# The DeltaNet layer's opening re-ordered: gate sums directly behind the first k projection, modulation moved behind the first N, and a and b projected in four column groups

## Chip, core and metric

The kernel runs on one core of a Trainium2 chip. The metric is the device time of one execution in microseconds (us), lower is better. A core has five instruction queues that run side by side and meet only at semaphores: PE (TensorE, matrix multiplications; "PEld" is its weight load), DVE (VectorE), ACT (ScalarE), POOL (GpSimd) and SP (SyncE, which only issues DMAs here). All data and all matrix products are float32.

## What is computed

Two layers over 256 latent tokens and 256 context tokens of width 1024. Layer 0 mixes by pooling, layer 1 by a bidirectional gated DeltaNet; each is followed by a mixture of experts. Every sub-layer is scaled, shifted and gated by a modulation vector. What the change touches is the entry into layer 1:

```python
def modulation(cvec, w_mod, b_mod):
    m = jax.nn.silu(cvec) @ w_mod + b_mod          # 1024 -> 6 * 1024, for each layer
    return jnp.split(m, 6, axis=-1)

def gdn_mixer(h, w_in, conv_w, a_log, dt_bias, ...):
    proj = h @ w_in                                # q, k, v, z: 1024 wide each; a, b: 16 each
    qkv = short_conv(proj[..., :3072], conv_w)     # 5 taps along the tokens, then SiLU
    g = -jnp.exp(a_log) * jax.nn.softplus(a + dt_bias)
    beta = jax.nn.sigmoid(b)
    ...                                            # per head and direction, in chunks:
    g = jnp.cumsum(g, -1)
    decay = exp(where(tril, g[i] - g[j], -inf))
    A = where(strict, (k * beta) @ k.T * decay, 0)
    sol = triangular_solve(eye + A, rhs)           # the inverse that the kernel builds
    ...                                            # then a recurrence over the chunks
```

There are 8 heads and 2 directions; the kernel works in 4 chunks of 128 tokens, so it inverts 8 triangular 128x128 systems for each head.

## The kernel before

**One head of the DeltaNet.** A head goes through: projections of k, v, q and z (`pe_project(h, j)` with j = 0 for k, 1 for v, 2 for q; `pe_project_z`), convolution (`dve_conv`), SiLU (`act_conv`), k times k transposed and k turned into rows (`pe_keys`), the exponents of the decays (`dve_n_args`, line 1189) and their Exp (`act_exp_n`, line 1196), the product N (`dve_n`, line 1232). N's diagonal 32x32 blocks are copied out (line 1239 on DVE, 1247 on ACT), sent to memory and read back in another layout by SP (`sp_blocks_out`, line 1004; `sp_blocks_in`, lines 1008 and 1010), and inverted row by row on POOL (`pool_invert`, lines 1033 to 1040). The result goes to memory and back (`sp_inverse_out`, line 1014; `sp_inverse_in`, line 1021), DVE and ACT place it (lines 1317 and 1358), and PE joins the blocks to inverses of 64 and 128 (`pe_join32`, line 1329, and what follows), after which the recurrence over the chunks runs (`pe_recur`).

**Steps.** Heads are pipelined by a step number x. Each engine has a function for a step (`pe_step`, `act_step`, `dve_step`, `sp_step`). In step x the engines make head x+1 up to its N and, beside it, close head x (join, recurrence). Step -1 makes head 0 alone; on PE it is not `pe_step` but a list of calls written out in the block at the end. PE's step 0 begins with the v projection of head 1 (`pe_project(1, 1)`), and everything there comes before the join of head 0. The order on each engine is the order in which the code is written; nothing re-orders it.

**Before the steps.** `pe_dn_setup` turns the modulated rows into columns `m.hT`, projects a and b (line 1710: 8 matmuls over the contraction in 8 parts, each 32 output rows wide and 512 tokens long), ACT copies the result (line 1738), PE turns it back to tokens in rows (line 1714). DVE and ACT form the gates (lines 1775 to 1784 and 1740 to 1745). `pe_dn_cumulate` sums them along the tokens by three matmuls (line 1721), DVE reads the sums (lines 1788 to 1800), PE turns them (line 1725), ACT copies them (line 1749), SP writes them to memory (line 1853) and reads them back spread over all partitions as `along` (line 996). `dve_n_args` needs `along`.

**Modulation.** The modulation of a layer is made in 3 groups q of 2048 columns, each in 8 parts k. For each part SP loads 1 MB of weights into a ring slot (`sp_mod`, line 239), PE multiplies in four column groups of 32 (`pe_mod`, line 251: 4 matmuls), DVE adds the bias (`dve_mod`, line 268), PE spreads the vector over the partitions (`pe_mod_spread`, line 262: 4 matmuls in banks 1 and 2) and ACT copies it (`act_mod`, line 274). The last two groups are q = NQ+1 and q = NQ+2 (NQ is 3). For q = NQ+2 only ring slots 4 and 5 are free, so part k+2 is loaded only when PE has used part k (`mod_before`). PE begins step 0 only when all copies are made, since the joins use banks 1 and 2:

```python
            pe_mod_spread(pe, NQ + 2, 1)
            pe.wait_ge(s("mod_ready"), 2 * NCH)
            for x in range(HEADS + 1):
                pe_step(pe, x)
```

SP, after step -1, waits until all modulation matmuls are done before it loads the second half of the output weights (line 1861) and only then comes to step 0, whose first act is the store of head 0's inverse.

## Time and profile before

| | us |
|---|---|
| median of 3 runs | 1050.08 (1046.65 to 1051.48) |
| the profiled execution | 1047.63 |
| its span in the profile | 1045.8 |
| PE busy | 810.4 (77%) |
| PE weight load busy | 482.5 (46%) |
| DVE busy | 428.5 (41%) |
| POOL busy | 384.2 (37%) |
| ACT busy | 330.1 (32%) |

The profiled execution takes 1.8 us more than its span, and 2.5 us less than the median. PE is the busiest engine, but the program has stages with different limits, so the shares of the whole span say little about one stage. The stage in question lies between about 398 us (columns `m.hT` ready) and 540 us (blocks of head 2 leave for memory). A timeline row gives the start in us, the duration in us, engine, line, operation, operands and, in brackets, the idle time before it and what ended it. PE splits each float32 matmul into two records, so x16 there is 8 matmuls.

### The profile page before, as it was taken

Reading aid. Unit: us, or ns where it says so; the run is one execution under the profiler, and the core shown is the slowest. Engines: PE = TensorE matmul, PEld = TensorE weight load, DVE = VectorE, ACT = ScalarE, POOL = GpSimd, SP = SyncE. Lnnn points to the kernel's source line nnn. Section 1 sums busy time; section 2 is a strip of 40 time slices with the busy share of each in tenths; the row PEclk is TensorE's granted clock in tenths of the full one; section 3 lists DMA queues with packets and bytes.
Section 4 is the critical chain, followed back from the end, with each engine's and each line's share of the span. In section 5 each row is a group of like instructions: output and inputs, shape, how many; then the busy total and the mean of one; then the engine's idle time right before and its main releaser. Section 6 shows DMA issues by size and latency. Waiting matters only on the chain.

```text
span 1045.8 us, 14887 instructions
## 1 busy us (share of the span) xinstructions
PE 810.4 (77%) x5183; PEld 482.5 (46%) x5183; DVE 428.5 (41%) x1005; ACT 330.1 (32%) x760; POOL 384.2 (37%) x718
## 2 busy tenths in 40 slices
PE   4498655999999158687799989899856863999980
PEld 0255332555555013254566666666645432555540
DVE  0306651111111692153576665676643333111115
ACT  0131202222222214054374564654741012222221
POOL 0000771333333395016438346364370022533330
PEclk8599766999999568688798898998965876899995
DMA  9999199968593694645523515334220346799933
GB/s 355 343 418 396 43 398 367 382 246 291 214 379 134 259 348 146 229 122 168 137 41 102 138 20 126 72 76 137 41 82 10 121 180 263 259 376 383 381 127 121
DMA packets 113533, 220.44 MB, mean 211 GB/s; under 512 B 44469, under 2 KB 78589, under 8 KB 100543
## 3 DMA queue, kind: packets, MB, share of 16 engines
q1 hardware_dynamic: 101272, 199.71, 54.6%
q0 software_dynamic: 8224, 15.75, 4.5%
q10 hardware_dynamic: 3975, 4.16, 1.2%
q8 instruction: 38, 0.62, 0.2%
q14 instruction: 24, 0.20, 0.1%
HBM read 213.25 MB, written 17.33 MB: 220 GB/s over the span
## 4 chain that ended last, share of the span: by engine, by line
PE 38%; POOL 18%; DMA 15%; DVE 11%; issue 11%; ACT 3%; SPq 3%; ACTq 1%; DVEq 0%; POOLq 0%
PE banks L656 11%; POOL arena L1039 7%; POOL arena L1037 7%; PE banks L668 6%; DMA weight_ring<-in_w_mod_dram 4%; DMA inverted_blocks<-arena 3%; PE banks L1810 3%; PE banks L1057 3%; PE banks L637 3%; SPq L1010 2%; PE banks L251 2%; DMA arena<-blocks 2%; DMA blocks<-arena 2%; POOL x_rows L319 2%; PE banks L834 2%
## 5 line engine op out<-in xcount | busy, mean ns | idle before, releaser
L1057 PE MATMUL banks<-h_cols,weight_ring 128*128 128x512 f32 (+1 forms) x384 | 163.6, 558 | 1.5 <-ACT modulation L274 0.7
L759 POOL DMA_INDIRECT y_of_tokens<-arena,place_now x42 | 44.4, 1056 | 161.4 <-ACT arena L691 157.3
L715 DVE TENSOR_TENSOR arena<-arena,banks 128x128 f32<-128x128 f32 x42 | 12.1, 288 | 211.7 <-ACT arena L684 162.2
L251 PE MATMUL banks<-weight_ring,c_cols 128*32 128x512 f32 x384 | 64.4, 776 | 42.4 <-DMA weight_ring<-in_w_mod_dram 42.2
L1057 PEld LDWEIGHTS banks<-h_cols,weight_ring 128*128 128x128 f32 x384 | 71.7, 204 | 40.4 <-issue 35.3
L1039 POOL TENSOR_TENSOR arena<-arena 128x60 f32<-128x60 f32 (+10 forms) x240 | 79.7, 332 | 18.8
L1037 POOL TENSOR_TENSOR arena<-arena 128x60 f32<-128x60 f32 (+10 forms) x240 | 76.9, 320 | 18.8
L735 POOL DMA_INDIRECT arena<-h_of_tokens,row_now x50 | 48.5, 970 | 69.4 <-POOL row_now L762 22.8
L679 ACT COPY arena<-arena 64x1024 f32<-64x1024 f32 x46 | 48.1, 1045 | 76.3 <-PE banks L637 54.1
L725 POOL DMA_DIRECT2D h_of_tokens<-h_rows x6 | 3.9, 646 | 183.1 <-DVE h_rows L307 183.1
L1033 POOL TENSOR_TENSOR arena<-arena,const 128x256 f32<-128x256 f32 x8 | 6.7, 843 | 168.6 <-DMA arena<-blocks 168.6
L656 PE MATMUL banks<-weight_ring,arena 128*64 128x256 f32 x544 | 66.6, 401 | 2.3 <-ACT arena L679 2.3
L637 PE MATMUL banks<-const,arena 64*128 64x64 f32 x352 | 57.0, 285 | 12.4 <-ACT arena L679 12.4
L637 PEld LDWEIGHTS banks<-const,arena 64*128 64x128 f32 x352 | 45.2, 198 | 35.3 <-issue 21.0
L656 PEld LDWEIGHTS banks<-weight_ring,arena 128*64 128x64 f32 x544 | 41.1, 145 | 31.1 <-issue 8.3
L684 ACT ACTIVATE arena<-banks 128x128 f32<-128x128 f32 x42 | 11.7, 278 | 127.1 <-PE banks L656 127.1
L319 POOL TENSOR_SCALAR x_rows<-x_rows,small 128x1024 f32<-128x1024 f32 x10 | 46.2, 4618 | 13.4 <-DVE small L301 13.0
L251 PEld LDWEIGHTS banks<-weight_ring,c_cols 128*32 128x32 f32 x384 | 9.9, 122 | 84.6 <-DMA weight_ring<-in_w_mod_dram 44.7
L709 DVE COPY arena<-banks 128x512 f32<-128x512 f32 x44 | 30.4, 691 | 35.6 <-PE banks L637 35.4
L1098 DVE SCALAR_TENSOR_TENSOR h_rows<-arena,h_rows 128x512 f32<-128x512 f32 (+1 forms) x64 | 41.0, 640 | 1.6
L274 ACT COPY modulation<-banks 128x512 f32<-128x512 f32 x24 | 13.1, 587 | 73.0 <-PE banks L262 37.9
L691 ACT COPY arena<-banks 128x512 f32<-128x512 f32 x42 | 24.6, 587 | 32.9 <-PE banks L668 32.9
(283 smaller groups left out, 1550.6 us busy)
## 6 DMA issues: line engine op xcount, KB each, us to landing
weight_ring<-in_w_mod_dram SPq DMA_DIRECT2D x48, 1024.0 KB, 10.8
weight_ring<-in_dn_w_in_dram SPq DMA_DIRECT2D x32, 512.0 KB, 7.1
weight_ring<-in_w_gate_dram SPq DMA_DIRECT2D x14, 1024.0 KB
weight_ring<-in_w_up_dram SPq DMA_DIRECT2D x14, 1024.0 KB
weight_ring<-in_w_down_dram SPq DMA_DIRECT2D x14, 1024.0 KB
arena<-in_w_gate_dram SPq DMA_DIRECT2D x6, 1024.0 KB
arena<-in_w_up_dram SPq DMA_DIRECT2D x6, 1024.0 KB
arena<-in_w_down_dram SPq DMA_DIRECT2D x6, 1024.0 KB
```

Source lines behind the costliest of these rows:

```text
L251: mm = pe.matmul(m.ps[j * COL:(j + 1) * COL, 0, :], m.c_cols[:, k, :], w[:, j, :], start=(k == 0), stop=(k == KD - 1))
L319: pool.tensor_scalar(x, x, v.mean_var[:, n % 4, 0:1], v.rstd[:, n % 4:n % 4 + 1], ALU.subtract, ALU.mult).then_inc(s("ln_gained"), 1)
L637: mm = pe.transpose(m.ps[:, B_TURN, k * TILE:(k + 1) * TILE], v.rows[:, k, :], v.ident[0:TILE, 0:TILE])
L656: mm = pe.matmul(column_half(B_GU, h)[:, 0:2 * P], v.slots_T[:, k, :], gate_up(slot, k)[:, :, h * P:(h + 1) * P], start=(k == 0), stop=(k ...
L668: mm = pe.matmul(column_half(B_DOWN, h), v.hidden[:, f, :], down(slot, f)[:, h * BANK:(h + 1) * BANK], start=(f == 0), stop=(f == FC - 1))
L679: act.copy(v.rows_flat, v.rows_in[u]).then_inc(s(t_ + "rows_copied"), 1)
L735: pool.indirect_dma_start(v.rows_in[u], None, h_dram, bass.IndirectOffsetOnAxis(m.row_now[:, at:at + 1], 0), bounds_check=last_token, oob_ ...
L759: pool.indirect_dma_start(y_halves, bass.IndirectOffsetOnAxis(m.place_now[:, u:u + 1], 0), v.y_tile[u], None, bounds_check=last_row, oob_i ...
L1037: then(pool.tensor_tensor(part, U[:, 0:q, j:j + 1].to_broadcast([P, q, BLK - 1 - j]), M[:, j, j + 1:BLK].unsqueeze(1).to_broadcast([P, q, ...
L1039: then(pool.tensor_tensor(U[:, 0:q, j + 1:BLK], U[:, 0:q, j + 1:BLK], part, ALU.subtract))
L1057: mm = pe.matmul(bank(6 + j % 2)[:, 0:CTX + SEQ - n0], head_w[h % 2][:, j, k, :], m.hT[:, k, n0:CTX + SEQ], start=(k == 0), stop=(k == KD ...
L1098: ins = dve.scalar_tensor_tensor(out=out, in0=src, scalar=tap, in1=out, op0=ALU.mult, op1=ALU.add)
```

## The change

Seven edits, all in the opening of layer 1:

- a and b: the 8 contraction parts are spread over four column groups of 32, so that each group sums two parts in its own 32 of the 128 output rows. The copy then takes 128 rows, and the turning back is a matmul with a new 128x32 constant that adds the four groups.
- The matmuls of the gate sums stand directly behind head 0's k projection, and the turning of the sums behind two more matmuls (of the v projection).
- `pe_keys(0)` stands inside the v projection, behind its part 5.
- The spread of group NQ+1 and the parts of group NQ+2 move behind: parts 0 and 1 before the z projection, 2 and 3 behind head 0's values, the spread of NQ+1 behind head 1's k projection, and parts 4 to 7 behind that.
- SP loads parts 2 to 7 of group NQ+2 after head 0's blocks have landed, no longer before and around the gate rows.
- ACT makes the copies of group NQ+1 after step -1, and in step -1 the copy of v's projection (`act_pad(0, 1)`) behind the Exp of N's exponents.
- DVE makes the convolution of head 0's k before N's exponents.

The order on PE, from the projection of a and b to the first keys of head 1. Line 251 is a modulation part (4 matmuls each), 262 the spread, 1057 a projection (128x512 for k and v, 128x256 for q), 1066 z, 1721 and 1725 the gate sums, 1111 and 1116 the keys, 1138 the values. Before:

```order
L1710 MATMUL banks<-h_cols,dn_inputs 32x512 x8
L1714 MATMUL banks<-const,arena 128x32 x4
L1057 MATMUL banks<-h_cols,weight_ring 128x512 x8
L262 MATMUL banks<-mod_sums,const 128x512 x4
L251 MATMUL banks<-weight_ring,c_cols 32x512 x8
L1057 MATMUL banks<-h_cols,weight_ring 128x512 x8
L251 MATMUL banks<-weight_ring,c_cols 32x512 x8
L1721 MATMUL banks<-arena,const 128x64 x3
L1725 MATMUL banks<-const,arena 64x128
L251 MATMUL banks<-weight_ring,c_cols 32x512 x8
L1111 MATMUL banks<-const,arena 128x128 x4
L1116 MATMUL banks<-arena 128x128 x4
```

The same stretch of PE now (lines are one to seven higher: 1715 is 1710, 1727 is 1721, 1732 is 1725, 1112 is 1111):

```order
L1715 MATMUL banks<-h_cols,dn_inputs 32x512 x8
L1720 MATMUL banks<-const,arena 128x32 x4
L1058 MATMUL banks<-h_cols,weight_ring 128x512 x8
L1727 MATMUL banks<-arena,const 128x64 x3
L1058 MATMUL banks<-h_cols,weight_ring 128x512 x2
L1732 MATMUL banks<-const,arena 64x128
L1058 MATMUL banks<-h_cols,weight_ring 128x512 x3
L1112 MATMUL banks<-const,arena 128x128 x4
L1117 MATMUL banks<-arena 128x128 x4
L1058 MATMUL banks<-h_cols,weight_ring 128x512 x3
```

Between the k projection and the gate sums stood a spread, two modulation parts, the v projection and two more parts; now nothing does.

The end of PE's opening, from the values of head 0 to the beginning of step 0 (the five matmuls of line 1057, now 1058), before:

```order
L1138 MATMUL banks<-const,h_rows 128x128 x4
L1057 MATMUL banks<-h_cols,weight_ring 128x512 x8
L262 MATMUL banks<-mod_sums,const 128x512 x4
L1057 MATMUL banks<-h_cols,weight_ring 128x512 x5
L1111 MATMUL banks<-const,arena 128x128 x4
```

and now:

```order
L1139 MATMUL banks<-const,h_rows 128x128 x4
L252 MATMUL banks<-weight_ring,c_cols 32x512 x8
L1058 MATMUL banks<-h_cols,weight_ring 128x512 x8
L263 MATMUL banks<-mod_sums,const 128x512 x4
L252 MATMUL banks<-weight_ring,c_cols 32x512 x16
L263 MATMUL banks<-mod_sums,const 128x512 x4
L1058 MATMUL banks<-h_cols,weight_ring 128x512 x5
```

Six of the eight parts of group NQ+2 and a second spread now stand here, ahead of step 0.

SP around the same place (1004 to 1010 are the blocks of head 0, 996 is `along`, 991 the weights of head 2), before:

```order
L239 DMA weight_ring<-in_w_mod_dram 128x2048 [waits mod_mm] x4
L1853 DMA decay_rows<-arena 2x8x128 [waits dn_setup_rows]
L1853 DMA decay_rows<-arena 2x8x128 x3
L996 DMA x_rows<-decay_rows 128x1024 [waits x_moved,gc_rows]
L996 DMA x_rows<-decay_rows 128x1024
L239 DMA weight_ring<-in_w_mod_dram 128x2048 [waits mod_mm] x2
L1004 DMA blocks<-arena 128x8x32 [waits k_length,n_mat]
L1008 DMA arena<-blocks 128x8x32 [waits n_out]
L1010 DMA arena<-blocks 32x1024 x4
L991 DMA weight_ring<-in_dn_w_in_dram 128x8x128 [waits proj,m_in]
```

and now:

```order
L1859 DMA decay_rows<-arena 2x8x128 [waits dn_setup_rows]
L1859 DMA decay_rows<-arena 2x8x128 x3
L997 DMA x_rows<-decay_rows 128x1024 [waits x_moved,gc_rows]
L997 DMA x_rows<-decay_rows 128x1024
L1005 DMA blocks<-arena 128x8x32 [waits k_length,n_mat]
L1009 DMA arena<-blocks 128x8x32 [waits n_out]
L1011 DMA arena<-blocks 32x1024 x4
L240 DMA weight_ring<-in_w_mod_dram 128x2048 [waits mod_mm,m_in]
L240 DMA weight_ring<-in_w_mod_dram 128x2048 [waits mod_mm] x5
L992 DMA weight_ring<-in_dn_w_in_dram 128x8x128 [waits proj]
```

The six weight loads moved from in front of and behind the gate rows to behind the landing of the blocks (`m_in`).

The diff, cut to its core:

```diff
+    v.add_groups = c[:, C_SLOT * P + 96:C_SLOT * P + 128]
...
-        abT = exp_q.rearrange("p d n -> p (d n)")[0:2 * NV, :]
+        abT = exp_q.rearrange("p d n -> p (d n)")
...
                 sp.wait_ge(s("m_in"), 80 * (x + 2))
+            if x < 0:
+                sp_mod(sp, NQ + 2, 2, KD)
...
             if x < 0:
-                act_pad(act, x + 1, 1)
                 act_squares_k(act, x + 1)
                 act_exp_n(act, x + 1)
+                act_pad(act, x + 1, 1)
...
         def dve_step(dve, x):
-            if x < 0:
-                dve_n_args(dve, 0)
             if closed(x):
                 dve_q_args(dve, x)
             if made(x):
                 dve_conv(dve, x + 1, 0)
+            if x < 0:
+                dve_n_args(dve, 0)
...
-            for k in range(KD):
-                mm = pe.matmul(m.ps[0:2 * NV, 3, :], w_ab[:, k, :], m.hT[:, k, :], start=(k == 0), stop=(k == KD - 1))
+            for r in range(2):
+                for g in range(4):
+                    mm = pe.matmul(m.ps[g * 2 * NV:(g + 1) * 2 * NV, 3, :], w_ab[:, 4 * r + g, :], m.hT[:, 4 * r + g, :],
+                                   start=(r == 0), stop=(r == 1))
             mm.then_inc(s("dn_setup_mm"), 1)
             pe.wait_ge(s("dn_setup_rows"), 2)
             for t in range(TT):
-                mm = pe.transpose(bank(4)[:, t * 2 * NV:(t + 1) * 2 * NV], abT[:, t * P:(t + 1) * P],
-                                  v.ident[0:2 * NV, 0:2 * NV])
+                mm = pe.matmul(bank(4)[:, t * 2 * NV:(t + 1) * 2 * NV], abT[:, t * P:(t + 1) * P], v.add_groups,
+                               start=True, stop=True)
...
-        def pe_dn_cumulate(pe):
+        def pe_dn_cumulate(pe, beside):
...
             mm.then_inc(s("dn_setup_mm"), 1)
+            beside()
             pe.wait_ge(s("dn_gates"), 4)
...
-            act.copy(abT, m.ps[0:2 * NV, 3, :]).then_inc(s("dn_setup_rows"), 1)
+            act.copy(abT, m.ps[:, 3, :]).then_inc(s("dn_setup_rows"), 1)
...
-            sp_mod(sp, NQ + 2, 2, 6)
             sp.wait_ge(s("dn_setup_rows"), 3)
...
-            sp_mod(sp, NQ + 2, 6, KD)
             sp_step(sp, -1)
...
             act_dn_setup(act)
-            act_mod(act, NQ + 1)
...
             ln_loads(act, 1, 0)
+            act_mod(act, NQ + 1)
             act_mod(act, NQ + 2)
...
             pe_dn_setup(pe)
             pe_project(pe, 0, 0)
-            pe_mod_spread(pe, NQ + 1, 1)
+            pe_dn_cumulate(pe, lambda: pe_project(pe, 0, 1, 0, 2))
+            pe_project(pe, 0, 1, 2, V_FIRST)
+            pe_keys(pe, 0)
+            pe_project(pe, 0, 1, V_FIRST, KD)
             for k in (0, 1):
-                pe_mod(pe, NQ + 2, k)
-            pe_project(pe, 0, 1)
-            for k in (2, 3):
-                pe_mod(pe, NQ + 2, k)
-            pe_dn_cumulate(pe)
-            for k in (4, 5):
-                pe_mod(pe, NQ + 2, k)
-            pe_keys(pe, 0)
-            for k in (6, 7):
                 pe_mod(pe, NQ + 2, k)
             pe_project_z(pe, 0)
             pe_project(pe, 0, 2)
             pe_values(pe, 0)
+            for k in (2, 3):
+                pe_mod(pe, NQ + 2, k)
             pe_project(pe, 1, 0)
+            pe_mod_spread(pe, NQ + 1, 1)
+            for k in range(4, KD):
+                pe_mod(pe, NQ + 2, k)
             pe_mod_spread(pe, NQ + 2, 1)
             pe.wait_ge(s("mod_ready"), 2 * NCH)
...
+    c[:, C_SLOT * P + 96:C_SLOT * P + 128] = i % 32 == np.arange(32)[None, :]
```

## Rows read from the trace of the kernel before

**Rows 1.** Waits, 384 to 510 us: engine, line, releaser: total us, times, longest

```profile
DVE arena L1788 <- PE banks L1721: 19.1, 1, 19.1
```

**Rows 2.** Timeline of PE in the setup: start us, duration us, line, operands, records

```profile
398.39 7.05 PE L1710 MATMUL banks<-h_cols,dn_inputs 128*32 128x512 f32 x16
406.11 0.43 PE L1714 MATMUL banks<-const,arena 32*128 32x32 f32 x4 [0.67 <-ACT arena L1738]
406.47 7.13 PE L1057 MATMUL banks<-h_cols,weight_ring 128*128 128x512 f32 x16
...
429.07 1.93 PE L251 MATMUL banks<-weight_ring,c_cols 128*32 128x512 f32 x16
430.93 0.88 PE L1721 MATMUL banks<-arena,const 128*128 128x64 f32 x6
```

**Rows 3.** Timeline of DVE, the gates and the bias sum of group NQ+2

```profile
412.47 0.22 DVE L1782 SCALAR_TENSOR_TENSOR arena<-arena,dn_inputs 128x64 f32<-128x64 f32 x1
...
465.80 0.69 DVE L268 TENSOR_TENSOR mod_sums<-banks,mod_sums 128x512 f32<-128x512 f32 x1
```

**Rows 4.** Timeline of ACT: after the last setup Exp, and head 1's diagonal

```profile
435.15 1.28 ACT L1103 ACT_TABLE_LOAD   x1
...
485.72 0.81 ACT L1247 COPY arena<-arena 32x256 f32<-32x256 f32 x2
```

**Rows 5.** The chain that ended last, 340 to 500 us: start us, us, what

```profile
431.92 0.20 DVE arena L1788
...
442.56 1.66 DVE arena L1189 x8
444.21 0.41 DVE arena L1095
...
447.79 0.64 ACT arena L1103
...
452.56 0.64 ACT arena L1196
...
456.40 2.28 DMA blocks<-arena
...
465.80 0.74 POOL arena L1033
```

**Rows 6.** Timeline of PE from the v projection to the join of head 0

```profile
420.87 8.27 PE L1057 MATMUL banks<-h_cols,weight_ring 128*128 128x512 f32 x16
...
437.62 1.94 PE L251 MATMUL banks<-weight_ring,c_cols 128*32 128x512 f32 x8 [0.55 <-DMA weight_ring<-in_w_mod_dram]
...
470.13 1.13 PE L262 MATMUL banks<-mod_sums,const 2*128 2x512 f32 x4
471.93 1.61 PE L262 MATMUL banks<-mod_sums,const 2*128 2x512 f32 x4 [0.67 <-ACT modulation L274]
474.21 6.25 PE L1057 MATMUL banks<-h_cols,weight_ring 128*128 128x512 f32 x10 [0.68 <-ACT modulation L274]
...
488.73 1.89 PE L1057 MATMUL banks<-h_cols,weight_ring 128*128 128x256 f32 x8
501.07 1.06 PE L1329 MATMUL banks<-arena 32*32 32x32 f32 x32 [10.46 <-DVE arena L1317]
```

**Rows 7.** Issue to landing of line 239's loads, 418 to 442 us

```profile
DMA to landing us min/median/max: 4.8/6.5/9.4
```

**Rows 8.** Issue to landing of line 1861's load, second half of output weights

```profile
DMA to landing us min/median/max: 13.4/13.4/13.4
```

**Rows 9.** Timeline of SP's queue: inverse of head 0 out; blocks of heads 1, 2

```profile
491.89 0.56 SPq L1014 DMA_DIRECT2D inverted_blocks<-arena  x1
...
497.19 0.52 SPq L1004 DMA_DIRECT2D blocks<-arena  x1
...
539.04 1.45 SPq L1004 DMA_DIRECT2D blocks<-arena  x1
```

**Rows 10.** Stretch at the beginning of step 0: length, PE busy, PE clock, DMA, GB/s

```profile
472.00:476.00 4.00, 3.33 (x7) 0.80 1.14 331
```

## The prediction

> **What bounds the kernel now.** I read the waits first. DVE sat idle 19.1 us for the gate sums [rows 1], the longest wait of PE, DVE or ACT in this opening. The timeline of PE shows why: the sums (line 1721) stand at 430.93, though the gates they need were finished at 412.7 (DVE line 1782, 412.47 + 0.22) [rows 2, 3]. In between PE did a spread, two modulation parts, the v projection and two more parts. Then the chain of waits: from the first reading of the sums (431.92) it runs without a gap over `along` (442.56), the convolution of k (444.21), its SiLU (447.79), the Exps (452.56) and the blocks of head 0 (456.40) to POOL's first inversion (465.80) [rows 5]. POOL is done 26.1 us later (491.89) [rows 9], and PE, which had finished all it could do at 490.62, waits 10.46 us for head 0's inverse until 501.07 [rows 6]. So before that join the bound is the path to N and POOL, not PE. Two things leave this stage: blocks of head 1 at 497.19 and of head 2 at 539.04 [rows 9]; from there on the loop over heads repeats. What the change is worth is how much earlier the blocks of head 2 leave.
>
> **Part 1, a and b in column groups.** Before, 8 matmuls in 7.05 us. The modulation parts have this very shape and use four column groups: two parts, that is 8 matmuls, took 1.93 us [rows 2]. So 5.1 us are saved. The copy has four times the partitions and the same 512 elements in each, so it costs the same. Turning back took 0.43 us for four; three matmuls with a full 128x128 stationary took 0.88 [rows 2], so four take 1.1 to 1.2: 0.7 us lost. Net 4.4 us: head 0's k projection starts at 406.47 - 4.4 = 402.1 and ends 7.1 later, at 409.2; the gates are ready at 412.7 - 4.4 = 408.3, before that.
>
> **Part 2, sums behind k, up to POOL.** Sums at 409.2 to 410.1, first reading 410.2 instead of 431.92: 21.7 us earlier. Two v matmuls (0.9 each) stand before their turning and end 0.25 after DVE's results are due, so `along` follows at 410.2 + 0.25 + (442.56 - 431.92 = 10.64) = 421.1. The convolution of k no longer waits for that: it starts when ACT's setup Exps are done, which was at 435.15 [rows 4] and is now at 413.7, and takes 3.6 (444.21 to 447.79). SiLU at 417.3, and by the old distance of 4.8 us over keys and squares ACT is free for the Exps at 422.0. N's exponents take 1.65 us for eight from 421.1, the first four 0.8: 421.9. Both paths meet at 422.0. From the Exps to the blocks it was 3.84 us, now 0.4 more because two small DVE operations stand behind the exponents: 426.2. POOL 9.4 later: 435.6. Both are 30.2 earlier than before [rows 5]. That the v copy stands later on ACT costs nothing: its projection ends at about 423, and the z projection, which needs the copy, comes only after two modulation parts.
>
> **Part 3, the modulation now in the way.** The 30 us do not reach the end, because PE may not begin step 0 until all modulation is copied. SP loads parts 2 to 7 only after the blocks have landed, at 435.6; PE has by then done its values (about 436.5) and waits. With two slots the loads come in pairs: the first needs 4.8 us when nothing is queued [rows 7], the second lands 2.5 later (0.55 idle behind a part of 1.94) [rows 6]. Step by step: parts 2 and 3 landed 442.9; part 3 multiplied 1.9: 444.8; head 1's k projection 8.3, taking the row that was partly at 1.2 GHz [rows 6]: 453.1; the first spread 3.4 on PE (470.13 to 473.54) [rows 6]: 456.5; part 4 (its load came beside the projection) 1.0: 457.5; only now can part 6 be loaded, 4.8, and part 7, 2.5: 464.8; part 7 multiplied 1.9: 466.7; bias sum 0.8 with its hand-over [rows 3]; the last spread with copies 4.1 (470.13 to 474.21) [rows 6], with 0.4 added as PE will be at the lower clock: step 0 at 472.0. Before it was 474.21. So PE gains only 2.2 us there; six loads that were hidden now stand in a row.
>
> **Part 4, what comes out.** PE's work in step 0 up to the join took 16.4 us (474.21 to 490.62) [rows 6] and will be ready at 488.4. Head 0's inverse: POOL done 435.6 + 26.1 = 461.7; SP is held by its wait for all modulation (466.7) and the issue of the output weights (1.7), so the store goes at 468.5. It came back to a placed inverse 9.2 us after its issue (491.89 to 501.07) [rows 6, 9]: 477.7, before 488.4. PE no longer waits, so the 10.46 us go as well. From the join to the blocks of head 2 is 37.97 us: 526.4. The other path is head 1's: its diagonal was ready 12.3 us after the beginning of step 0 (485.72 + 0.81 - 474.21) [rows 4, 6], now at 484.3, and the blocks of head 2 follow 41.85 us behind those of head 1 (497.19 to 539.04) [rows 9]: 526.2. Both give 12.6 to 12.8 us. I take 1 us off for the clock: before, it was at 0.80 of full speed at the beginning of step 0 [rows 10] after dense work; now PE has been waiting for loads.
>
> Of that clock the Trainium skill ("TensorE: Matmul & The Clock Gate", Part 1) says that the slow state is the default and activity releases it. By that rule alone the five projection matmuls that open step 0 would run wholly at the low clock.
>
> The price from rows: 6.25 us before [rows 6], of which the low clock was a part; eight at full clock took 7.13 [rows 2], so five take 4.4 at 2.4 GHz and 8.9 at 1.2 GHz. All low would cost 2.6 us more than before, the full clock would return 1.8. I take 1.
>
> **SP's queue.** The store of head 0's inverse moves behind a freshly issued load of 2 MB, which took 13.4 us from issue to landing when head weights were queued ahead of it [rows 8], as they are now. If the store waits all of it: 466.7 + 13.4 = 480.1, plus at most the 9.2 = 489.3: PE's join waits 0.9 us. Head 1's blocks go right behind the reload, at about 485 to 486 rather than 484.3. So 1 us, 2 at most.
>
> The Trainium skill ("DMA: Bandwidth & Descriptors", Queues, rings and completion order) has descriptors of a ring consumed in order and the semaphore write only after every earlier write of that DMA engine. By it the sum would be a gain of about 10.6, by the rows of an unloaded queue 11.6; no row of the kernel before has this store behind a load.
>
> **Sum.** 12.6 - 1 = 11.6 us. Against the profiled execution: 1047.6 - 11.6 = 1036.0. The median lies 2.5 above it: 1050.1 - 11.6 = 1038.5.
>
> **Rivals.**
> 1. PE warm and loads short. If PE is at 2.4 GHz from part 3 on, the k projection takes 7.1 and nothing is added in step 0: 1.2 + 0.4 + 1 + 1.8 = 4.4 us more, a gain of 16: 1034. For it: even with a spread's waits just behind it, the clock at the beginning of step 0 was still 0.80 [rows 10]; against: it now waits three times for loads. Chance 0.14.
> 2. Column groups do not overlap. Then the 5.1 us return and pass through the whole path to step 0: gain 6.5, 1043.5. Against it stand the modulation parts with the same shape. Chance 0.03. With the store held longer than I take it, or the k projection and spreads at the low clock throughout (14 instead of 8.3 for the projection), the gain is likewise 5 to 8, 1042 to 1045: chance 0.11.
> 3. The gain is eaten inside the head loop. The two paths in part 4 are within 0.2 us of each other, so any delay on one of them counts in full, and what came for free in PE's idle 10.46 us (head 1's v convolution on DVE, for one) is now beside the join. If half of it returns: gain 1 to 5, 1045 to 1049. Chance 0.1.
> 4. Slower: the loads in pairs. Each pair stands on PE's path to step 0 with 7.3 us. The break-even is a step 0 at 472.0 + 11.6 = 483.6, that is 5.8 us more for each of the two pairs. The longest landing in the quiet stretch was 9.4 [rows 7]; the 13.4 of the big load is the bound from above [rows 8]. With 13.4 in place of 4.8, twice: 17.2 later, 5.6 us slower than before: 1055.7. Against: nothing else is in the queue when parts 2 and 3 are issued, and only head 2's weights follow parts 6 and 7. Chance 0.07.
> 5. As forecast, gain 8 to 15: 1035 to 1042. Chance 0.55.
>
> **Range and chances.** 1032 to 1046 takes in rivals 1 and 2 and the 2.4 us by which single runs lie off the median; it leaves out rival 4 and most of 3. A measurement of this kernel can tell about 0.5%, 5.25 us, from no change. Faster by more than that: forecast, rival 1, most of 2: 0.82. Within: the rest of 2 and 3: 0.12. Slower: 0.06, most of rival 4.
>
> **What the profile of the changed kernel would show.** Lines 1715 (a, b) 1.9 us; sums (1727) at 410; blocks of head 0 at 426, POOL at 436; PE idle before modulation parts 2 and 3 (about 4 us) and 6 and 7 (about 5); step 0's first projection at 472; the join of head 0 at 488 to 490 with hardly a wait; blocks of head 2 at 526 to 528. It would be wrong if step 0 began at 460 (loads not in the way) or behind 478, or if the join still waited for POOL.

## The result, and the profile after

Seven runs of each kernel: 1037.05 us median (1035.06 to 1041.88) after the change, 1050.08 before; the ratio is 0.9895 with a 95% interval of 0.9867 to 0.9923. The profiled execution took 1036.18 us, its span is 1034.4, so 11.4 less than before. The forecast was 1038.5, and 1036.0 for the profiled execution. One of the seven runs before, of 1109.33 us, was a slow one: it counts in that median but not in the ratio, and without it the median is 1049.19. So the gain is 11.0 us by the ratio, which compares means, and 12.1 to 13.0 by medians.

Where it came from is read on three stages. PE turned the conv weights, the last thing that is the same in both kernels, at 398.13 before and at 400.13 now: the part ahead, which no edit touches, was 2.0 us longer in this execution (398.6 to 403.4 in the other profiles; there is only one profile of the kernel before). From there to the leaving of head 2's blocks it took 140.9 us before and 130.7 now, 10.2 less. The rest of the head loop and the tail behind it gave 3.2 more (506.8 and 503.6 us), of which nothing was forecast and nothing was edited. All positions below are counted from that turning, so that kernels can be compared.

The timeline of PE in the changed kernel (start, duration, line, operands, records; idle time and its end in brackets). It answers to [rows 2] and [rows 6]:

```profile
400.13 0.32 PE L1711 MATMUL banks<-const,dn_inputs 120*128 120x120 f32 x1 [0.85 <-ACT h_cols L1740]
400.38 1.93 PE L1715 MATMUL banks<-h_cols,dn_inputs 128*32 128x512 f32 x16
403.01 1.08 PE L1720 MATMUL banks<-const,arena 128*128 128x32 f32 x8 [0.71 <-ACT arena L1745]
...
410.88 0.78 PE L1727 MATMUL banks<-arena,const 128*128 128x64 f32 x6
...
441.87 1.93 PE L252 MATMUL banks<-weight_ring,c_cols 128*32 128x512 f32 x8 [4.88 <-DMA weight_ring<-in_w_mod_dram]
...
445.92 7.13 PE L1058 MATMUL banks<-h_cols,weight_ring 128*128 128x512 f32 x16
...
456.77 3.64 PE L252 MATMUL banks<-weight_ring,c_cols 128*32 128x512 f32 x16
463.99 1.93 PE L252 MATMUL banks<-weight_ring,c_cols 128*32 128x512 f32 x8 [3.58 <-DMA weight_ring<-in_w_mod_dram]
468.05 1.93 PE L252 MATMUL banks<-weight_ring,c_cols 128*32 128x512 f32 x8 [2.13 <-DMA weight_ring<-in_w_mod_dram]
470.80 2.08 PE L263 MATMUL banks<-mod_sums,const 2*128 2x512 f32 x4 [0.81 <-DVE mod_sums L269]
473.54 2.56 PE L263 MATMUL banks<-mod_sums,const 2*128 2x512 f32 x4 [0.67 <-ACT modulation L275]
476.78 5.99 PE L1058 MATMUL banks<-h_cols,weight_ring 128*128 128x512 f32 x10 [0.68 <-ACT modulation L275]
...
492.85 0.69 PE L1330 MATMUL banks<-arena 32*32 32x32 f32 x32
```

The four column groups do run together: 8 matmuls in 1.93 us where it was 7.05. The gate sums stand at 410.88. The modulation parts at 441.87, 463.99 and 468.05 wait for loads: of the six parts from 441.87 on, four wait for their own load. Step 0 begins at 476.78, 76.6 from the turning, where it was 76.1 before, so PE gained nothing there. The join of head 0 (line 1330) has no bracket; the wait of 10.46 us of [rows 6] is gone.

SP's queue in the same stretch (start, time to issue, line), which answers to [rows 9]:

```profile
427.81 0.37 SPq L1005 DMA_DIRECT2D blocks<-arena  x1
...
436.84 23.96 SPq L240 DMA_DIRECT2D weight_ring<-in_w_mod_dram  x6
460.85 8.78 SPq L992 DMA_DIRECT2D weight_ring<-in_dn_w_in_dram  x4
470.05 1.35 SPq L1866 DMA_DIRECT2D weight_ring<-in_dn_w_out_dram  x1
471.44 0.56 SPq L1015 DMA_DIRECT2D inverted_blocks<-arena  x1
483.26 0.36 SPq L1022 DMA_DIRECT2D arena<-inverted_blocks  x1
488.91 0.37 SPq L1005 DMA_DIRECT2D blocks<-arena  x1
...
530.85 0.53 SPq L1005 DMA_DIRECT2D blocks<-arena  x1
```

Counted from the turning, head 0's blocks leave 30.6 us earlier (27.7 against 58.3), head 1's only 10.3 (88.8 against 99.1) and head 2's 10.2 (130.7 against 140.9). The six modulation loads take SP from 436.84 to 460.80. The store of the inverse is issued at 471.44, and its landing, which lets the reload go, comes at 483.26.

The clock, in four stretches of the windows view (length, busy PE and records, clock as a share of 2.4 GHz, DMA share, GB/s):

```profile
452.00:456.00 4.00, 3.33 (x11) 0.98 0.35 139
456.00:460.00 4.00, 4.00 (x17) 0.50 0.47 150
460.00:464.00 4.00, 0.42 (x5) 0.50 0.92 315
...
472.00:476.00 4.00, 3.33 (x8) 0.50 1.03 340
```

From about 456 to 478 the granted clock is 1.2 GHz. It fell behind the first spread, while PE was still at work: parts 4 and 5 (456.77) take 3.64 us instead of 1.93, and the first wait for a load behind them comes only at 460.4. So it is not the waits for parts 6 and 7 that brought it down.

### The profile page after: what moved, and what is told of

Read it like the earlier page. It is cut to its first block and busy times, and to the rows that moved or that the text cites. A ratio compares the mean times of both kernels' runs of the same rounds, so it can differ in the third digit from the quotient of the medians.

```text
span 1034.4 us, 14895 instructions
## 1 busy us (share of the span) xinstructions
PE 802.5 (78%) x5187; PEld 479.6 (46%) x5187; DVE 430.4 (42%) x1005; ACT 330.2 (32%) x760; POOL 380.1 (37%) x718
## 5 line engine op out<-in xcount | busy, mean ns | idle before, releaser
L716 DVE TENSOR_TENSOR arena<-arena,banks 128x128 f32<-128x128 f32 x42 | 12.1, 288 | 212.4 <-ACT arena L685 212.4
L1040 POOL TENSOR_TENSOR arena<-arena 128x60 f32<-128x60 f32 (+10 forms) x240 | 78.0, 325 | 18.8
L1038 POOL TENSOR_TENSOR arena<-arena 128x60 f32<-128x60 f32 (+10 forms) x240 | 75.9, 316 | 18.8
L657 PE MATMUL banks<-weight_ring,arena 128*64 128x256 f32 x544 | 65.4, 396 | 2.3 <-ACT arena L680 2.3
L252 PEld LDWEIGHTS banks<-weight_ring,c_cols 128*32 128x32 f32 x384 | 9.8, 123 | 94.9 <-DMA weight_ring<-in_w_mod_dram 55.1
L710 DVE COPY arena<-banks 128x512 f32<-128x512 f32 x44 | 30.5, 692 | 35.4 <-PE banks L638 35.4
L269 DVE TENSOR_TENSOR mod_sums<-banks,mod_sums 128x512 f32<-128x512 f32 x6 | 4.1, 680 | 78.4 <-PE banks L252 78.4
## 6 DMA issues: line engine op xcount, KB each, us to landing
weight_ring<-in_w_mod_dram SPq DMA_DIRECT2D x48, 1024.0 KB, 10.5
arena<-in_w_up_dram SPq DMA_DIRECT2D x6, 1024.0 KB, 11.4
```

Of the source, the lines that this page charges most:

```text
L252: mm = pe.matmul(m.ps[j * COL:(j + 1) * COL, 0, :], m.c_cols[:, k, :], w[:, j, :], start=(k == 0), stop=(k == KD - 1))
L657: mm = pe.matmul(column_half(B_GU, h)[:, 0:2 * P], v.slots_T[:, k, :], gate_up(slot, k)[:, :, h * P:(h + 1) * P], start=(k == 0), stop=(k ...
L1038: then(pool.tensor_tensor(part, U[:, 0:q, j:j + 1].to_broadcast([P, q, BLK - 1 - j]), M[:, j, j + 1:BLK].unsqueeze(1).to_broadcast([P, q, ...
L1040: then(pool.tensor_tensor(U[:, 0:q, j + 1:BLK], U[:, 0:q, j + 1:BLK], part, ALU.subtract))
```

## The experiments

The theory: there is one path, from a and b over the gate sums, `along`, N and the blocks of head 0 to the pairs of modulation loads behind them, step 0, the join and the blocks of head 2. Rivals: parts of it have slack (then an edit on it gives little), POOL and the store set the join, or the clock sets step 0. The edits on ACT and the new place of head 0's keys were not tried by themselves. The table has the positions of all kernels in us from the turning of the conv weights, read from their timelines, and the times; a ratio is to the kernel before in the same session.

| kernel | gate sums | blocks 0 | step 0 | join 0 | blocks 1 | blocks 2 | median us | ratio (interval) |
|---|---|---|---|---|---|---|---|---|
| before | 32.8 | 58.3 | 76.1 | 102.9 | 99.1 | 140.9 | 1050.08 | |
| changed | 10.8 | 27.7 | 76.6 | 92.7 | 88.8 | 130.7 | 1037.05 | 0.9895 (0.9867 to 0.9923) |
| e11, changed again | 12.6 | 28.7 | 77.8 | 95.0 | 91.1 | 131.7 | 1040.26 | 0.9910 (0.9889 to 0.9930) |
| e1, undivided | 15.3 | 31.4 | 80.2 | 96.3 | 92.4 | 132.8 | 1037.33 | 0.9917 (0.9887 to 0.9947) |
| e12, undivided again | 15.3 | 31.2 | 79.6 | 96.0 | 92.1 | 132.5 | 1042.49 | 0.9941 (0.9919 to 0.9963) |
| e2, groups alone | 26.8 | 52.2 | 69.4 | 96.6 | 92.8 | 136.9 | 1041.58 | 0.9929 (0.9889 to 0.9969) |
| e3, exponents first | 10.7 | 35.4 | 83.7 | 101.4 | 97.5 | 139.1 | 1046.76 | 0.9997 (0.9983 to 1.0012) |
| e4, pair early | 12.6 | 29.2 | 70.1 | 87.6 | 83.7 | 124.8 | 1029.96 | 0.9827 (0.9794 to 0.9861) |
| e5, parts forward | 12.6 | 28.6 | 67.9 | 84.6 | 80.7 | 122.3 | 1027.65 | 0.9798 (0.9752 to 0.9843) |
| e6, store first | 12.6 | 28.8 | 77.7 | 94.9 | 90.9 | 131.3 | 1037.18 | 0.9894 (0.9853 to 0.9935) |
| e7, e5 and store first | 10.7 | 26.8 | 65.4 | 82.0 | 78.1 | 118.5 | 1029.07 | 0.9824 (0.9785 to 0.9863) |
| e8, gaps filled | 12.6 | 29.0 | - | 90.8 | 86.8 | 128.0 | 1034.87 | 0.9888 (0.9845 to 0.9931) |
| e9, k of head 1 ahead | 12.6 | 28.6 | 64.8 | 76.4 | 72.0 | 113.3 | 1022.18 | 0.9729 (0.9707 to 0.9752) |
| e10, e9 and store first | 12.6 | 28.8 | 65.0 | 75.7 | 72.2 | 116.4 | 1022.06 | 0.9744 (0.9718 to 0.9770) |

Four sessions are in it: the changed kernel's own, e1 to e4, e5 to e8, and e9 to e12 each ran beside the kernel before (1050.08, 1047.44, 1047.15 and 1048.73 us).

**e1 and e12, a and b undivided in the changed kernel.**

```diff
-            for r in range(2):
-                for g in range(4):
-                    mm = pe.matmul(m.ps[g * 2 * NV:(g + 1) * 2 * NV, 3, :], w_ab[:, 4 * r + g, :], m.hT[:, 4 * r + g, :], ...)
+            for k in range(KD):
+                mm = pe.matmul(m.ps[0:2 * NV, 3, :], w_ab[:, k, :], m.hT[:, k, :], ...)
```

> The changed kernel with a and b projected again by eight matmuls into one group of 32 rows. Theory (one path: a and b, gate sums, along, N, blocks of head 0, weight loads in pairs, step 0, join): the projection takes 7.1 us again instead of 1.9 and the turning back 0.4 instead of 1.1, so everything behind comes 4.4 us later: blocks of head 0 leave 31.8 us after the conv weights are turned instead of 27.7, step 0 and the blocks of head 2 are 4 to 5 us later, the time is 1041 (changed kernel about 1037), ratio to before 0.991 to 0.995. Rival (step 0 is set by the clock and the weight loads, not by what comes before them): blocks of head 0 are 4.4 later, step 0 less than 2, the time 1037 to 1038.

> The changed kernel with a and b projected undivided, once more and beside the changed kernel on the same chip. Theory (the saving of 4.4 us passes through the whole path): 3 to 4.5 us slower than the changed kernel. Rival (half of it is lost on the way, as the first pair of profiles with 2.1 us at the blocks of head 2 suggests, because another path sets them): 0 to 2 us slower.

In e1 sums and blocks 0 come 4.5 and 3.7 us later than in the changed kernel's first profile, about as the theory has it, step 0 3.6, but the blocks of head 2 only 2.1, and the time is 1037.33 where 1041 was expected. Beside the changed kernel in one session (e11, e12), it is 2.7 at the sums, 2.6 at blocks 0, 1.9 at step 0 and 0.8 at blocks 2, and the medians differ by 2.2 us, between the theory's 3 and the rival's 2, with intervals that overlap. So the full 4.4 us do not pass. One reason is seen in e11's timeline of PE:

```profile
401.42 0.46 PE L1711 MATMUL banks<-const,dn_inputs 120*128 120x120 f32 x1 [0.74 <-ACT h_cols L1740]
401.81 3.64 PE L1715 MATMUL banks<-h_cols,dn_inputs 128*32 128x512 f32 x16
```

The same eight matmuls take 3.64 us here and 1.93 in the changed kernel's first profile. The windows view of e11 has the clock at 0.50 there:

```profile
402.00:404.00 2.00, 2.00 (x12) 0.50 0.28 115
```

In the table every kernel with groups, in the changed order, has its sums either at about 10.7 or at 12.6, the second in seven of ten profiles; with a and b undivided they stand at 15.3 in both. The rest shrinks at two places that have nothing to do with a and b. In the first pair it is the way from head 1's blocks out to POOL's start, 10.8 us in the changed kernel and 9.1 in e1. In the second it is the clock: the five matmuls that open step 0 took 7.17 us in e11 and 6.27 in e12. Single profiles of one kernel differ by as much as this edit brings.

**e11, the changed kernel again.**

> The changed kernel once more, beside the next one. Both theories: 1036 to 1038, ratio to before 0.989 to 0.991. In its first profile the way from head 1's blocks out to POOL's start took 10.8 us, against 9.1 to 9.6 in the other profiles; theory (a delay of that one execution, since nothing in the program is queued there): 9.1 to 9.6 here.

Its ratio agrees (0.9910 against 0.9895), though the time lies above the 1036 to 1038 expected. From blocks 1 out to POOL's start it took 9.4 us here and 10.8 in the first profile, so that delay is not in every execution; e5's profile has it too (10.5).

**e2, the groups in the kernel before.** The same edit on a and b, the other way round, and nothing else.

> The kernel before with only a and b in four column groups, no other edit. Theory: PE worked without a pause from the projection of a and b to the gate sums, so the 4.4 us saved pass to the sums, to N, to POOL (which sets the join there) and to the end: 1045.5, ratio 0.995 to 0.997. Rival (the weight loads of parts 2 to 5, which depend on PE, or the copies of x, set the sums): less than 1.5 us, ratio 0.999 or more.

More came than expected: sums 6.0 us earlier, step 0 6.7, blocks 2 4.0, and 5.9 us in the median. But only 2.7 of the 6.0 us at the sums are the edit's own work: here too the eight matmuls ran at the low clock (3.64 us). The other 3.3 us come behind it. The v projection takes 7.13 instead of the 8.27 of [rows 6], the modulation parts before it 1.92 instead of 3.64, and the spread ahead of them is 0.4 shorter:

```profile
416.87 1.92 PE L252 MATMUL banks<-weight_ring,c_cols 128*32 128x512 f32 x16
418.72 7.13 PE L1058 MATMUL banks<-h_cols,weight_ring 128*128 128x512 f32 x16
```

PE stood at 2.4 GHz there and at 1.2 in part before. Whether the edit brought that or the execution is not shown: there is one profile of each kernel, and e2's is of its slowest run (1046.77). So the 4.0 us at blocks 2 can't be put down to the groups as such. In time the two halves do not add up: re-ordering alone is 0.9917 and 0.9941 (e1, e12), groups alone 0.9929, both 0.9895 and 0.9910.

**e3, DVE's order as before.**

```diff
         def dve_step(dve, x):
+            if x < 0:
+                dve_n_args(dve, 0)
...
-            if x < 0:
-                dve_n_args(dve, 0)
```

> The changed kernel with DVE's order in step -1 as before: N's exponents ahead of the convolution of head 0's k. Theory: DVE waits for along first (421.9 in the changed kernel), then 1.7 us of exponents and 3.6 of convolution, SiLU at 427.2 instead of 418.7; the Exps about 8 us later, blocks of head 0 about 8 later (436 instead of 427.8), and all of it passes through the weight loads to step 0 and the blocks of head 2: time 1044 to 1046. Rival (a slack of some us between blocks of head 0 and step 0): 1037 to 1041.

The theory holds in full: blocks 0 come 7.7 us later, step 0 7.1, blocks 2 8.4, the median is 1046.8, and nothing is left of the gain. DVE's timeline shows why (the exponents after a wait for `along`, then the convolution behind them):

```profile
424.94 1.66 DVE L1190 TENSOR_SCALAR arena<-x_rows,arena 128x128 f32<-128x128 f32 x8 [7.15 <-DMA x_rows<-decay_rows]
426.51 0.48 DVE L1096 TENSOR_SCALAR arena<-arena 128x512 f32<-128x512 f32 x1
```

Without that small edit the earlier sums would have bought only a longer wait.

**e4, the loads of parts 2 and 3 ahead of the blocks.**

```diff
             if x < 0:
-                sp_mod(sp, NQ + 2, 2, KD)
+                sp_mod(sp, NQ + 2, 4, KD)
...
                 sp_along(sp, h)
+            sp_mod(sp, NQ + 2, 2, 4)
             sp_step(sp, -1)
```

> The changed kernel with one edit on SP: the loads of modulation parts 2 and 3 are issued behind along, ahead of the blocks of head 0, and only parts 4 to 7 behind the landing of the blocks. PE's order is untouched. Theory (the loads in pairs set step 0): parts 2 and 3 land before PE has done the values of head 0, PE's wait of 4.9 us and the one between the two parts go, parts 4 and 5 are loaded under head 1's k projection; step 0 begins 4 to 7 us earlier, the blocks of head 0 leave at most 0.5 us later because SP waits for part 1, and the blocks of head 2 and the end are 4 to 6 us earlier: 1031 to 1033, ratio to before 0.982 to 0.985. Rival (POOL and SP set the blocks of head 2, since there they left 3 us after the diagonal was ready): the time stays at 1036 to 1037.

Step 0 comes 6.5 us earlier than in the changed kernel's first profile, blocks 2 5.9, the ratio is 0.9827; the time, 1029.96, is 1 us better than expected. PE's timeline: parts 2 and 3 no longer wait, 6 and 7 still do.

```profile
438.19 1.92 PE L252 MATMUL banks<-weight_ring,c_cols 128*32 128x512 f32 x16
...
458.29 1.93 PE L252 MATMUL banks<-weight_ring,c_cols 128*32 128x512 f32 x8 [3.26 <-DMA weight_ring<-in_w_mod_dram]
462.04 1.94 PE L252 MATMUL banks<-weight_ring,c_cols 128*32 128x512 f32 x8 [1.82 <-DMA weight_ring<-in_w_mod_dram]
```

The loads were not free for the blocks: those of head 0 took 7.1 us from issue to the first reload (429.88 to 436.93) instead of 2.3, and POOL began 43.3 us from the turning instead of 36.8. It cost nothing, since the join was not waiting for POOL. That also rules out POOL as the bound of the changed kernel.

**e5 and e7, modulation drawn further forward.** On top of e4: parts 0 and 1 before head 0's keys, 2 and 3 before z, 4 and 5 before the spread of NQ+1. In e7 also the second half of the output weights behind head 0's store and reload.

> The changed kernel with the modulation drawn forward where PE and the DMA queue are idle: parts 0 and 1 on PE ahead of head 0's keys (PE waited 3.3 us there), the loads of parts 2 and 3 on SP behind along, parts 2 and 3 on PE ahead of the z projection, parts 4 and 5 ahead of the spread of group NQ+1. Theory (step 0 is set by blocks landed, then a pair of loads, each pair 7 to 8 us; two pairs before, one and a hidden one now): counted from the turning of the conv weights, blocks of head 0 leave at 27.5 to 29.5 as before, step 0 begins at 59 to 62 instead of 76.6, head 0's inverse is stored at about 62 and placed by 73, the join is ready on PE at 76 and hardly waits, blocks of head 2 leave at 114 to 117 instead of 130.7: time 1021 to 1024, ratio to before 0.973 to 0.978. Rival (POOL, the store behind 4 MB of weights, or the small packets of the blocks now set the join and head 1's blocks): join at 85 or later, blocks of head 2 at 122 to 128: 1029 to 1034.

> The edits of the two kernels above together (modulation parts drawn forward, and the output weights behind the store). Theory: with step 0 some 16 us earlier the store is closer to the path; it lands 4 to 6 us earlier than without this edit and the join, if it waits at all there, waits less: 0 to 3 us faster than the parts alone, 1019 to 1023. Rival (the weights of head 2, not the output weights, hold the store): no difference between the two.

Both missed, e5's time by 4 us or more and e7's by 6: step 0 of e5 stands at 67.9 instead of 59 to 62, and its join (84.6) and blocks 2 (122.3) are where the rival had them. I had not costed what parts 2 and 3 do where I put them. They wait 2.28 and 1.02 us for their loads, and z behind them took 5.06 us instead of 3.84, partly at the low clock. That is 4.5 us; the rest is not settled.

```profile
428.53 1.67 PE L252 MATMUL banks<-weight_ring,c_cols 128*32 128x512 f32 x8 [2.28 <-DMA weight_ring<-in_w_mod_dram]
431.22 1.94 PE L252 MATMUL banks<-weight_ring,c_cols 128*32 128x512 f32 x8 [1.02 <-DMA weight_ring<-in_w_mod_dram]
433.08 5.06 PE L1067 MATMUL banks<-weight_ring,h_cols 128*128 128x128 f32 x32
```

The median of e5 is 2.3 us below e4's, in another session, and the intervals overlap. e7 is no faster than e5. Most of its earlier marks comes from its one profile: the sums stand at 10.7, 1.9 us earlier, and head 1's blocks reach POOL in 9.0 us instead of 10.5. The store did land sooner (8.1 us after its issue, 11.6 in e5), so the output weights do hold it, but nothing waited for that.

**e6, the store ahead of the output weights.**

```diff
-            sp.wait_ge(s("mod_mm"), 2 * KD * NQ)
-            sp.dma_start(w_out[1], ...).then_inc(s("w_out"), 16)
...
                 sp_inverse_out(sp, x)
                 sp_inverse_in(sp, x)
+                if x == 0:
+                    sp.wait_ge(s("mod_mm"), 2 * KD * NQ)
+                    sp.dma_start(w_out[1], ...).then_inc(s("w_out"), 16)
```

> The changed kernel with the load of the second half of the output weights (2 MB) issued behind the store and reload of head 0's inverse instead of ahead of them. Theory: the store's landing, 11.8 us from its issue in the changed kernel against 4.8 before, falls to 5 to 7, since only head 2's weights are queued ahead; the reload is issued 5 us earlier; but neither was on the path (DVE and PE were not ready), so join and blocks of head 1 stay within 0.5 us and the time at 1036 to 1038. Rival (the store behind the weights is what costs the 3 us between the ready diagonal of head 2 and its leaving): 1033 to 1034.

As the theory had it: the time is the same. In SP's queue the store lands 7.1 us after its issue, with only head 2's weights ahead:

```profile
473.15 0.56 SPq L1015 DMA_DIRECT2D inverted_blocks<-arena  x1
480.22 0.36 SPq L1022 DMA_DIRECT2D arena<-inverted_blocks  x1
```

It was 11.8 with both loads ahead (471.44 to 483.26 above; 10.3 in e11) and 4.8 before the change, when they had been issued 20 us earlier. So the queue's price is real, and off the path.

**e8, PE's gaps filled.** Head 1's first five v matmuls out of step 0 and into the waits for parts 6 and 7.

```diff
-                pe_project(pe, x + 1, 1, 0, V_FIRST)
+                if x > 0:
+                    pe_project(pe, x + 1, 1, 0, V_FIRST)
...
-            for k in range(4, KD):
+            for k in (4, 5):
                 pe_mod(pe, NQ + 2, k)
+            pe_project(pe, 1, 1, 0, 4)
+            pe_mod(pe, NQ + 2, 6)
+            pe_project(pe, 1, 1, 4, V_FIRST)
+            pe_mod(pe, NQ + 2, 7)
```

> The changed kernel with the five matmuls of head 1's v projection, which open step 0, moved into PE's waits for the loads of parts 6 and 7 (four behind part 5, one behind part 6); nothing else. Theory (the granted clock is a part of the price: 1.2 GHz from about 456 to 478 because PE waits there, and the last spread took 5.9 us instead of 4.1): the clock is at 2.4 GHz for part of that stretch, the last spread takes 4.1 to 5, step 0's remaining work begins 1 to 2 us earlier, keys of head 1 come when their SiLU is ready, 3 us behind the copies, not 5.8: blocks of head 1 and 2 leave 3 to 4 us earlier, time 1033 to 1034. Rival (the clock stays low, since the gaps are still there): the projection takes 8.9 us in the gaps, part 7 is late by 1 to 2 us, the gain is 0 to 2 us: 1035 to 1037.

In the windows view the stretch that was at 0.50 is now at full clock (compare 456 to 464 above):

```profile
456.00:460.00 4.00, 3.33 (x17) 1.00 0.56 221
460.00:464.00 4.00, 4.00 (x22) 1.00 0.70 223
...
472.00:476.00 4.00, 2.33 (x4) 0.50 1.15 334
```

This fits the theory but does not prove it. The first of these rows lies ahead of the first filled gap, where PE's order is still that of the changed kernel: parts 4 and 5 took 1.92 us here and 3.64, 3.19 and 3.02 in the profiles of the changed kernel, e11 and e6. So the clock was higher before the edit could act. And e9's stretch from 452 to 456, filled without a gap, is at the low clock:

```profile
452.00:456.00 4.00, 4.00 (x5) 0.50 1.01 422
```

In e8's timeline of PE parts 6 and 7 take 1.06 us each, where they took 1.93, and the last spread begins at its full rate. Then PE waits for the SiLU of head 1's k, which ends on ACT at 478.12:

```profile
465.55 1.06 PE L252 MATMUL banks<-weight_ring,c_cols 128*32 128x512 f32 x8 [0.48 <-DMA weight_ring<-in_w_mod_dram]
468.10 1.06 PE L252 MATMUL banks<-weight_ring,c_cols 128*32 128x512 f32 x8 [0.43 <-DMA weight_ring<-in_w_mod_dram]
469.98 1.13 PE L263 MATMUL banks<-mod_sums,const 2*128 2x512 f32 x4 [0.81 <-DVE mod_sums L269]
471.77 2.56 PE L263 MATMUL banks<-mod_sums,const 2*128 2x512 f32 x4 [0.67 <-ACT modulation L275]
478.22 1.09 PE L1112 MATMUL banks<-const,arena 128*128 128x128 f32 x4 [3.89 <-issue]
```

Blocks 2 leave 3.3 to 3.7 us earlier than in e6 and e11. In time the median is 2.3 us below that of e6, which ran beside it, but the ratios are 0.9888 and 0.9894 with intervals that overlap, so the gain is seen in one trace and not shown by the runs.

**e9 and e10, what follows from all of it.** On top of e4: parts 0 and 1 before head 0's keys, 2 and 3 left behind the values, 4 and 5 before the first spread, head 1's v matmuls in the gap before parts 6 and 7, and head 1's convolution, SiLU and keys ahead of the last spread.

```diff
             pe_project(pe, 1, 0)
+            for k in (4, 5):
+                pe_mod(pe, NQ + 2, k)
             pe_mod_spread(pe, NQ + 1, 1)
-            for k in range(4, KD):
+            pe_project(pe, 1, 1, 0, V_FIRST)
+            for k in (6, 7):
                 pe_mod(pe, NQ + 2, k)
+            pe_keys(pe, 1)
             pe_mod_spread(pe, NQ + 2, 1)
...
             act_mod(act, NQ + 1)
+            act_conv(act, 1, 0)
             act_mod(act, NQ + 2)
...
             dve_step(dve, -1)
+            dve_conv(dve, 1, 0)
             dve_mod(dve, NQ + 2)
```

> The changed kernel with what the runs so far point to: modulation parts 0 and 1 on PE ahead of head 0's keys, loads of parts 2 and 3 ahead of the blocks on SP, parts 4 and 5 ahead of the spread of group NQ+1, and, new, head 1's k and v drawn out of step 0: its v projection fills the wait for parts 6 and 7, its convolution and SiLU of k and its keys come before the last spread. Theory (what counts is how much PE work stands between the last load and the join, and the clock it runs at): PE reaches the join of head 0 about 11 us behind the last copies instead of 16, at about 72 to 76 from the turning of the conv weights (92.7 changed, 84.6 with the parts drawn forward); the store of head 0's inverse, queued behind 4 MB of weights, now sets the join and through SP's order the blocks of head 1, which leave at 72 to 75; blocks of head 2 at 114 to 117: time 1020 to 1023, ratio to before 0.974 to 0.978. Rival (POOL's inversion is slowed, or PE is held elsewhere in step 0): 1025 to 1028, no better than the parts alone.

> The kernel above with the second half of the output weights loaded behind the store and reload of head 0's inverse. Theory: here the store is on the path, so its landing 3 to 5 us earlier brings blocks of head 1 and the join 2 to 5 us forward: 1017 to 1021. Rival (head 2's weights, 2 MB in small packets just ahead of the store, hold it by themselves): 0 to 1 us.

e9 and e10 are the fastest. e9 has 1022.18 us and a ratio of 0.9729, against 0.9910 for the changed kernel in the same session. The positions came within 0.7 us of what was expected (join 76.4, blocks 1 at 72.0, blocks 2 at 113.3). The modulation parts behind head 1's work wait for no load any more, and the join waits 1 us again, for DVE:

```profile
446.58 2.07 PE L252 MATMUL banks<-weight_ring,c_cols 128*32 128x512 f32 x16
...
459.75 1.92 PE L252 MATMUL banks<-weight_ring,c_cols 128*32 128x512 f32 x16
...
478.84 0.69 PE L1330 MATMUL banks<-arena 32*32 32x32 f32 x32 [1.02 <-DVE arena L1318]
```

For e10 the rival's number was right, no gain over e9, and not its reason. The store landed 4.9 us after its issue where it took 8.1 in e9, so the output weights had held it, but the join came only 0.7 earlier. Blocks 1 leave when the diagonal is copied, in both (473.55 and 474.29), and now the moved load stands beside them: they took 6.1 us to their reload instead of 3.2, and blocks 2 left 3.0 us later than in e9. So the store was not what set blocks 1 in e9, as its expectation had it.

## Why the prediction was right, point by point

The forecast lay 1.4 us above the median and the mechanism is the one that was worked out, but its terms erred both ways. That the total came so near is in part luck.

- **Column groups** (part 1): 1.93 and 1.08 us, as put, in this profile. In e11 the first is 3.64. The step did not consider that these matmuls may stand at the low clock, as they did in seven of ten profiles; the gain of 4.4 us is then 2.7.
- **Sums to POOL** (part 2): sums forecast at 11.1 from the turning, measured 10.8; blocks 0 at 28.1, measured 27.7; POOL at 37.5, measured 36.8. e3 shows that the edit on DVE carries this step.
- **Modulation in the way** (part 3): right in kind, shown by e4, and 2.8 us too small: step 0 at 73.9, measured 76.6. Two terms were too large: the first pair was done 0.9 us sooner, and the k projection ran at full clock (7.13, put at 8.3). What was too small, in the terms of the sum: the first spread took 3.8 us, put at 3.4; part 4 ran at 1.2 GHz (3.64 for parts 4 and 5), which costs 0.8; part 7 landed 4.1 behind part 6, put at 2.5; the last spread with its copies took 5.9 (470.80 to 476.7), put at 4.5. The prediction took 2.5 from a pair of loads and left out that part 7's load is issued only when part 5 is done. That distance goes with the clock: it is 2.5 to 2.6 in e5, e7 and e8, where parts 4 and 5 took 1.92, and 3.6 to 4.2 in the seven profiles where they took 2.9 to 3.6. So the terms that failed are that distance and the clock from the first spread on, for which I took 0.4 us.
- **The clock in step 0**: I took 1 us off the gain because PE would come from waits and no longer from dense work at 0.80. That was a misreading: [rows 10] ends 1.8 us behind the beginning of step 0 (474.21) and is mostly of what lies ahead of it. The kernel before was already at the low clock there, in its own windows view:

```profile
474.00:478.00 4.00, 3.79 (x5) 0.57 1.06 394
```

The five matmuls took 6.25 us before, 5.99 in the changed kernel and 7.17 in e11, so the 1 us is not seen in the first profile and nearly is in the second. In neither did they run wholly at the low clock, which would be 8.9 (twice five eighths of the 7.13 of [rows 2]).

- **What comes out** (part 4): PE ready for the join 16.1 us behind step 0, put at 16.4 (17.2 in e11); the 10.46 us of idle time went whole. Blocks 2: 10.2 us earlier (9.2 in e11), forecast 11.6.
- **The store** (SP's queue): put at up to 13.4 us, measured 11.8 and 4.8 before, and 7.1 in e6 behind one load instead of two. By the rule of the Trainium skill that the prediction cites (a semaphore's write only after every earlier write), these rows agree. e6 shows that it cost nothing here.
- The missing 1.4 us were hidden by two things that no edit touches: 3.2 us gained in the later heads and the tail, and 2.0 lost ahead of the stage. Nothing in the prediction has them. From blocks 2 to the end it took 503.6 us in the changed kernel and 506.1 in e11, so most of this is scatter. But both kernels with the old order stand highest (506.8 before, 507.3 in e2; 502.2 to 506.4 in the twelve with the new order), so a small gain there may belong to the change. Its cause is open.

Of the rivals, the one in which column groups do not overlap is out (1.93 and 3.64 against 7.05). POOL and the store are out by e4 and e6. The faster rival (PE warm) had its first term, the k projection at 7.13, but not the full clock behind it. The one that lost the gain inside the head loop is out: the 10.3 us of head 1's blocks are still 10.2 at head 2's. The slower rival needed loads of 13.4 us; the changed kernel's took 5.0 to 7.5, as the trace's answer on line 240 has it for the stretch from 436 to 470 us:

```profile
DMA to landing us min/median/max: 5.0/5.9/7.5
```

## What to carry to other kernels

When work is moved out of the way, find who waits for it next: here 30.6 us of earlier blocks became 10.2, because step 0 waited for the moved modulation, and its loads stood in a row with their slots. Loads that need only a free slot belong ahead of a queue's next long wait, not behind it. And when an operation waits for data from memory, put the work that waits for nothing in front of it on the same engine; without that one exchange on DVE nothing of the gain was left (e3).

## What the runs showed that I had not expected

- The granted clock makes terms of this kernel vary by as much as some of the edits bring. Eight column-grouped matmuls took 1.93 us or 3.64 in the same program. The Trainium skill ("TensorE: Matmul & The Clock Gate", Part 1) has the low clock as the default that activity lifts; the trace of e8, at 1.00 while PE had no gap, agrees. But the level does not simply follow PE's work: it fell at 456 in the changed kernel with PE busy, it was 0.50 in e9's filled stretch, and in e11 it was 1.00 from 464 to 466 while PE did nothing. How much it adds to a stage one sees only over several profiles.
- POOL's inversion of head 0 took 23.4 us in the changed kernel (436.89 to 460.33) and 26.1 before [rows 5, 9]. In the trace of before, its operations take 0.69 to 0.73 us while DVE runs the convolution (471.38 to 474.5); those of 128x46 took 0.26 and 0.28 in the changed kernel, where DVE was not at it. First POOL, then DVE of the kernel before:

```profile
470.76 0.27 POOL L1037 TENSOR_TENSOR arena<-arena 128x48 f32<-128x48 f32 x1
471.11 0.38 POOL L1039 TENSOR_TENSOR arena<-arena 128x48 f32<-128x48 f32 x1
471.57 0.69 POOL L1037 TENSOR_TENSOR arena<-arena 128x46 f32<-128x46 f32 x1
472.33 0.73 POOL L1039 TENSOR_TENSOR arena<-arena 128x46 f32<-128x46 f32 x1
```

```profile
471.38 3.11 DVE L1098 SCALAR_TENSOR_TENSOR arena<-arena 128x512 f32<-128x512 f32 x4
```

That DVE slows POOL there is what these rows suggest; no run here tried it by itself. The Trainium skill ("SBUF — State Buffer", SBUF: two separate sides) names a pair of ports that DVE, reading two inputs in SBUF, and GpSimd hold in turn, each for a whole instruction. The rows agree with it in kind.
